# Depthwise convolution of a Conformer layer: three channel blocks on TensorE in place of four, and VectorE's taps dealt anew

## The chip, the cores and the metric

One NeuronCore of a Trainium2 chip runs the whole program as one launch. The metric is the device time of that launch in microseconds (us), the median of a few runs. The engines are TensorE (PE, with its weight loads PEld), VectorE (DVE), ScalarE (ACT), GpSimd (POOL) and SyncE (SP), which here only issues DMAs. Each engine has a queue of its own and works through it in order; engines wait for each other through semaphores.

## The reference

The program is one inference step of a two-layer decoder trunk for 512 prompt rows and 8 x 4 sample rows, 544 rows in all, 1024 channels wide, in float32. Layer 0 is a gated short convolution beside a dilated attention, layer 1 a Conformer convolution module, and each layer ends with a mixture of experts (32 experts, 2 per row). The change lies in the Conformer module:

```python
def odd_mixer(h, w_pw1, b_pw1, dw_w, dw_b, ln_g, ln_b, w_pw2, b_pw2, conv_buf):
    z = h @ w_pw1 + b_pw1
    za, zg = jnp.split(z, 2, axis=-1)
    u = za * jax.nn.sigmoid(zg)
    ctx = jnp.zeros((n, C_KERNEL - 1, C_WIDTH), u.dtype) if conv_buf is None else conv_buf.astype(u.dtype)
    u_ext = jnp.concatenate([ctx, u], axis=1)
    c = causal_dwconv(u_ext, dw_w) + dw_b          # 31 taps, each channel by itself
    c = jax.nn.silu(layer_norm(c, ln_g, ln_b))
    return c @ w_pw2 + b_pw2, u_ext[:, -(C_KERNEL - 1):]
```

## The kernel before

Channels lie on the 128 partitions in eight blocks of 128 (c = 0 to 7), rows along the free axis. The Conformer module follows the experts of layer 0 and the norm after them (`norm(2)`). It goes unit by unit, one unit for each channel block. All queues are written out by hand; nothing reorders them.

**A unit.** TensorE makes two products of 16 `mm` calls each (32 recorded matmuls): m = 2c, the gate, into psum banks 0 and 1, and m = 2c + 1, the value, into banks 2 and 3 (L1814; `z_done` counts them). Product m waits until the banks' earlier content is read: an even one for ScalarE's sigmoid of the unit before (L904, `sig_ready`), an odd one for VectorE's `glu` of the unit before (`u_ready`). `glu(c)` (L1333, L1335, L1337) writes the gated rows u of block c into `cu` (prompt) and `cs` (samples).

**The convolution of the 512 prompt rows** is done in one of two ways.

- *On VectorE*, for the blocks in `DVE_CONV`: ScalarE makes tap 0 with the bias (`first_tap`, L896), and `conv(c, lo, hi)` adds taps lo to hi - 1, one `scalar_tensor_tensor` over 128 x 512 for each (L1351), each waiting for the one before it. `DVE_TAPS[u]` says which taps VectorE does after `glu(u)`; after them it does `sample_sums(u)`, then `glu(u + 1)`.
- *On TensorE*, for the blocks in `PE_CONV`: GpSimd writes 31 small diagonal matrices (`make_diags`, L652), `conv_parts(n)` multiplies with them in 32 x 32 tiles into psum banks 4 to 7 (L1777, 248 recorded matmuls, `part_done`), ScalarE copies the four partial sums out (`keep_parts`, L885, 128 x 2048, `part_kept`), `fold_parts(n)` adds them (L1787, `pe_conv_done`), and ScalarE writes the result with the bias (`keep_pe_conv`, L890, `pe_conv_kept`).

**The sample rows** of every block: GpSimd multiplies windows by taps (L666), VectorE sums them (`sample_sums`, L1360, `sconv_summed`), ScalarE adds the bias (`keep_sconv`, L878).

**Order.** On TensorE, `conv_parts` stands after an even product m and `fold_parts` after product m + 1; the last block's convolution stands among the `mean` products. ScalarE's loop over units does, in this order: sigmoid of c, `keep_sconv(c - 1)`, then, where c is in `PART_AT`, `keep_parts`, then `first_tap(c)` for a VectorE block, then `keep_pe_conv`. After the loop: `keep_sconv(7)`, `keep_parts(3)`, `keep_pe_conv(3)`.

**After the units.** `mean(k)` (L1795) adds block k to the mean over channels in psum and waits for all of block k (`wait_conv`). `mean_done` lets VectorE subtract the mean (L1375); squares (ScalarE L924, GpSimd L672), `variance` (L1834), root, reciprocal, swish and the second projection (L1602) follow, then the norm, the router and the 32 experts of layer 1.

**SyncE** loads the first two expert weights of layer 1 into ring slots 0 and 1 once all products are done and `part_done` has reached `len(PE_CONV)` (L458), since the diagonal matrices lie in those slots.

Of the kernel before, what the change touches and what calls it, by code (L numbers as in the profile page):

```python
# [31 lines left out]
KD = D // P  # L32
# [18 lines left out]
MSLOTS = SLOTS + 2  # L51
PIECE = 1024
CK = 31
PE_CONV = (1, 4, 6, 7)
DVE_CONV = tuple(c for c in range(KD) if c not in PE_CONV)
PW1_SLOT = (2, 3, 0, 1)
LN_PART = ((256, TOK), (0, 256))
PW2_ORDER = (4, 2, 3, 0, 1)
PART_AT = (2, 5, 7)
DVE_TAPS = (((0, 1, 17),), ((0, 17, 31),), ((2, 1, 25),), ((2, 25, 31), (3, 1, 10)), ((3, 10, 25),),  # L60
            ((3, 25, 31), (5, 1, 19)), ((5, 19, 31),), ())
UP = SEQ + CK - 1
US = DEC_T + CK - 1
KEYS = [128, 256, 64]
# [65 lines left out]
def program(nc, x_in, w_mix0, kv_in, w_out, w_pw1, w_pw2, w_moe, smalls, consts, masks, rows, st_a, st_c,  # L130
            y_out, k_out, v_out, ua_p_out, ua_s_out, uc_p_out, uc_s_out):
    ctx = ExitStack()
    with ctx:
# [3 lines left out]
        def sem(name):  # L137
            return ctx.enter_context(nc.semaphore(name))
# [24 lines left out]
        psum = ctx.enter_context(nc.psum_tensor("psum", [P, 8, 512], F32))  # L163

        def view(off, n, pat=None, parts=P, **dims):
            a = ar[0:parts, off:off + n]
            return a.rearrange(pat, **dims) if pat else a

        ident = cst[:, C_ID:C_ID + P]
        mean_of = cst[:, C_MEAN:C_MEAN + P]  # L170

        def bcast(ap, shape):
            return ap.to_broadcast(shape)
# [65 lines left out]
        mean_done = sem("mean_done")  # L239
# [83 lines left out]
        cT = view(B_C, KD * TOK, "p (k t) -> p k t", k=KD)  # L323
# [63 lines left out]
        def diags(n):  # L387

            o = 4096 + CK * 32 * (n % 2)
            return ring[:, n // 2, o:o + CK * 32].rearrange("p (j c) -> p j c", j=CK)  # L390
# [4 lines left out]
        def wait_conv(eng, k):  # L395

            eng.wait_ge(sconv_kept, k + 1)
            if k in PE_CONV:
                eng.wait_ge(pe_conv_kept, PE_CONV.index(k) + 1)
            else:  # L400
                eng.wait_ge(conv_done, k + 1 - sum(c < k for c in PE_CONV))

# [21 lines left out]
        def _(sp):  # L424
# [19 lines left out]
            def experts(n):  # L444
                for u in (2, 0, 1, 3) if n == 0 else (0, 1, 2, 3):
# [6 lines left out]
                    elif u < 2:  # L452

                        sp.wait_ge(z_done, 2 * KD)
                        sp.wait_ge(part_done, len(PE_CONV))
                    else:
# [57 lines left out]
        def _(pool):  # L514
# [135 lines left out]
            def make_diags(n):  # L650
                o = V_DW + CK * PE_CONV[n]
                nc.gpsimd.tensor_tensor(diags(n), bcast(fold[:, None, :], [P, CK, 32]),  # L652
                                        bcast(sv[:, o:o + CK][:, :, None], [P, CK, 32]), ALU.mult
                                        ).then_inc(diag_made, 1)
# [23 lines left out]
        def _(act):  # L678
# [41 lines left out]
            for m in range(23):  # L720
# [8 lines left out]
                if m == 16:  # L729

                    for q in range(4):
                        t = nc.scalar.activation(vS[0:SAMPLES, 4, 192 * q:192 * q + 192],
                                                 psum[32 * q:32 * q + 32, b, 0:192], ACT.Copy)
# [141 lines left out]
            def keep_sconv(c):  # L875
                act.wait_ge(sconv_summed, c + 1)
                out = cT[:, c, SEQ:TOK]
                nc.scalar.activation(out, out, ACT.Identity, bias=sv[:, V_DWB + c:V_DWB + c + 1]  # L878
                                     ).then_inc(sconv_kept, 1)

            def keep_parts(n):
                act.wait_ge(part_done, n + 1)
                if n:
                    act.wait_ge(pe_conv_done, n)
                nc.scalar.activation(parts, psum[:, 4:8, :], ACT.Copy).then_inc(part_kept, 1)  # L885

            def keep_pe_conv(n):
                c = PE_CONV[n]
                act.wait_ge(pe_conv_done, n + 1)
                nc.scalar.activation(cT[:, c, 0:SEQ], psum[:, 4, :], ACT.Identity,  # L890
                                     bias=sv[:, V_DWB + c:V_DWB + c + 1]).then_inc(pe_conv_kept, 1)
# [8 lines left out]
            for c in range(KD):  # L900
# [5 lines left out]
                if c:  # L906
                    keep_sconv(c - 1)
                if c in PART_AT:
                    keep_parts(PART_AT.index(c))
                if c in DVE_CONV:  # L910
                    first_tap(c)
                if c in PART_AT:
                    keep_pe_conv(PART_AT.index(c))
            act.wait_ge(u_ready, KD)
            act.dma_start(brow, rows[0:1, :].to_broadcast([P, D])).then_inc(row_in, 16)
            keep_sconv(7)
            keep_parts(3)
            keep_pe_conv(3)

            sq = hT_of(2)  # L920
            lo, hi = LN_PART[0]
# [19 lines left out]
        def _(dve):  # L941
# [422 lines left out]
            for u in range(KD):  # L1364
                glu(u)
                for c, lo, hi in DVE_TAPS[u]:
                    conv(c, lo, hi)
# [41 lines left out]
        def _(pe):  # L1409
            mm, tr = nc.tensor.matmul, nc.tensor.transpose  # L1410
# [52 lines left out]
            for m in range(23):  # L1463
# [13 lines left out]
                if m == 16:  # L1477

                    for k in range(KD):
                        for q in range(4):  # L1480
                            t = mm(psum[32 * q:32 * q + 32, b, 0:192], hT[:, k, SEQ:TOK],
                                   w[:, k, 192 * q:192 * q + 192], start=k == 0, stop=k == KD - 1,
                                   tile_position=(0, 32 * q))
                elif 12 <= m < 16:
                    i = m - 12
                    for h in range(2):
                        for k in range(KD):
                            t = mm(psum[0:ROWS[i], b + h, 0:384], hT[:, k, P * i:P * i + ROWS[i]],  # L1488
                                   w[:, k, 384 * h:384 * h + 384], start=k == 0, stop=k == KD - 1)
                else:  # L1490
                    c = m % 6 if m < 12 else (4, 5, 2, 3, 0, 1)[m - 17]
                    for h in range(2):
                        for k in range(KD):
                            t = mm(psum[:, b + h, 0:HALF], w[:, k, P * c:P * c + P],  # L1494
                                   hT[:, k, HALF * h:HALF * h + HALF], start=k == 0, stop=k == KD - 1)
# [8 lines left out]
            for g in range(GROUPS):  # L1504
                t = tr(psum[0:32, 3, P * g:P * g + P], ps[:, CACHED + 32 * g:CACHED + 32 * g + 32], ident)
# [4 lines left out]
            for bb in range(2):  # L1510
                for s_, (rows_, g) in enumerate([(SAMPLES, g) for g in range(GROUPS)] + VT):
                    for q in range(4):
# [3 lines left out]
                        t = mm(psum[32 * q:32 * q + 32, 4 + bb, 0:256], w, v, start=s_ == 0,  # L1516
                               stop=s_ == GROUPS + 3, tile_position=(0, 32 * q))
            t.then_inc(so_done, 1)
            pe.wait_ge(so_sum, 1)
            for c in range(4):  # L1520
                t = tr(psum[:, 0, P * c:P * c + P], view(A_OS + P * c, P), ident)
# [45 lines left out]
            for n in range(16):  # L1567
# [7 lines left out]
                for t_ in range(w):  # L1575
                    t = tr(psum[:, 3 + t_ // 4, P * (t_ % 4):P * (t_ % 4) + P], sc[:, P * t_:P * t_ + P], ident)
# [190 lines left out]
            def conv_parts(n):  # L1767

                c = PE_CONV[n]
                pe.wait_ge(u_ready, c + 1)  # L1770
                pe.wait_ge(diag_made, n + 1)
                if n:
                    pe.wait_ge(pe_conv_kept, n)
                for j in range(CK):
                    s = j % 4
                    for i in range(4):
                        t = mm(psum[32 * s:32 * s + 32, 4 + i, :], diags(n)[32 * i:32 * i + 32, j, :],  # L1777
                               cu[32 * i:32 * i + 32, c, j:j + SEQ], start=j < 4, stop=j >= CK - 4,
                               tile_position=(32 * i, 32 * s))
                t.then_inc(part_done, 1)  # L1780

            def fold_parts(n):

                pe.wait_ge(fold_made, 1)
                pe.wait_ge(part_kept, n + 1)
                for i in range(4):
                    t = mm(psum[32 * i:32 * i + 32, 4, :], fold, parts[:, i, :], start=True, stop=True,  # L1787
                           tile_position=(0, 32 * i))
                t.then_inc(pe_conv_done, 1)

            def mean(k):

                wait_conv(pe, k)
                for h, (lo, hi) in enumerate(LN_PART):
                    t = mm(psum[:, h, 0:hi - lo], mean_of, cT[:, k, lo:hi], start=k == 0, stop=k == KD - 1)  # L1795
                return t

            for m in range(2 * KD):
                c, gate = m // 2, m % 2 == 0
                b = 2 * (m % 2)  # L1800
                if m % 4 == 0:
                    pe.wait_ge(dense_w[m // 4], 32)
                slot1 = PW1_SLOT[m // 4]
                if m >= 2:
                    p = m - 2
                    if p % 2 == 0:
                        pe.wait_ge(sig_ready, p // 2 + 1)
                    else:
                        pe.wait_ge(u_ready, p // 2 + 1)
                w = ring[:, slot1, 0:4096].rearrange("p (k c) -> p k c", k=KD)  # L1810
                o = (256 if gate else 0) + P * (c % 2)
                for h in range(2):
                    for k in range(KD):
                        t = mm(psum[:, b + h, 0:HALF], w[:, k, o:o + P], hT2[:, k, HALF * h:HALF * h + HALF],  # L1814
                               start=k == 0, stop=k == KD - 1)
                t.then_inc(z_done, 1)
                if m in (4, 10, 14):
                    conv_parts((4, 10, 14).index(m))
                if m in (5, 11, 15):
                    fold_parts((5, 11, 15).index(m))  # L1820

            pe.wait_ge(sig_ready, KD)
            for k in range(6):
                mean(k)
            conv_parts(3)
            mean(6)
            fold_parts(3)
            mean(7).then_inc(mean_done, 1)
            def variance(h):

                lo, hi = LN_PART[h]
# [147 lines left out]
```

## Time and profile before

| | |
|---|---|
| median of 3 runs | 1252.81 us (1250.18 to 1253.29) |
| the profiled execution | 1254.29 us, its span 1252.5 us, granted TensorE clock 0.939 |
| busy in the span | PE 1082.8 us, DVE 381.4 us, ACT 228.4 us, POOL 190.0 us |
| the first to the last product of the units | 658.9 to 811.7 us |
| VectorE begins to subtract the mean | 832.20 us |

Times in the rows are us from the start of the span; a row of a timeline gives the start, the duration, the engine, the line, the operation, what it writes and reads, and how many instructions are merged in it. In brackets stands for how long the engine was idle before the row, and whose end it then followed. Matmuls are pipelined and their ends are modelled.

### The profile page before, as it was taken

To read this page: it belongs to the slowest core of one execution; us is meant where nothing else is said; L and a number is where in the kernel's file an instruction comes from. 1 tells how busy PE (TensorE), PEld (TensorE's weight loads), DVE (VectorE), ACT (ScalarE), POOL (GpSimd) and SP (SyncE) were. 2 spreads that over 40 slices of the span, in tenths; PEclk is the share of its full clock that TensorE was granted. 3 is DMA by queue.
4 is the path that set the end of the run, shared out by engine and by line. 5 is a ranking of instruction groups with operands and counts; after the bars stand their busy time and mean duration, and the time that the engine had idled before them with its cause. 6 is when DMAs were issued, how large, how long until landed. Compare 5 with 4: busy or idle time off the path is not lost.

```text
span 1252.5 us, 18870 instructions
## 1 busy us (share of the span) xinstructions
PE 1082.8 (86%) x7107; PEld 681.9 (54%) x7108; DVE 381.4 (30%) x733; ACT 228.4 (18%) x413; POOL 190.0 (15%) x301
## 2 busy tenths in 40 slices
PE   5999998899869988888849999989959989798890
PEld 3887585676435544444438776754435545454440
DVE  2000003342351111111154899833262211111116
ACT  4000011344201111101140101144111111011112
POOL 0000010110013222111101211120004322232110
PEclk9999999899988999989979999999979999899895
DMA  9323032800455999999971110070095999989735
GB/s 363 167 95 140 9 117 70 301 2 5 158 220 194 409 408 409 408 405 408 379 286 36 69 67 1 3 259 21 33 391 178 408 408 398 364 330 407 292 151 229
DMA packets 72080, 281.74 MB, mean 225 GB/s; under 512 B 11775, under 2 KB 11839, under 8 KB 68737
## 3 DMA queue, kind: packets, MB, share of 16 engines
q1 hardware_dynamic: 55824, 251.66, 51.4%
q0 software_dynamic: 10960, 17.89, 4.1%
q10 hardware_dynamic: 5216, 11.10, 2.5%
q8 instruction: 54, 0.88, 0.3%
q14 instruction: 26, 0.20, 0.0%
HBM read 270.36 MB, written 29.65 MB: 240 GB/s over the span
## 4 chain that ended last, share of the span: by engine, by line
PE 56%; DMA 24%; DVE 12%; ACT 4%; issue 3%; DVEq 0%; POOL 0%; ACTq 0%; SPq 0%; POOLq 0%
DMA ring<-w_moe 15%; PE psum L1494 11%; PE psum L1683 8%; DMA ar<-w_moe 7%; PE psum L1602 5%; PE psum L1814 5%; DVE ar L1351 4%; PE psum L1738 4%; PE psum L1488 3%; PE psum L1777 3%; PE psum L1711 2%; PE psum L1545 2%; PE psum L1561 1%; PE psum L1666 1%; DVE ar L1138 1%
## 5 line engine op out<-in xcount | busy, mean ns | idle before, releaser
L1683 PE MATMUL psum<-ring,ar 128*64 128x256 f32 x1408 | 179.0, 400 | 21.1 <-DMA ring<-w_moe 19.3
L1683 PEld LDWEIGHTS psum<-ring,ar 128*64 128x64 f32 x1408 | 102.3, 143 | 95.2 <-issue 31.2
L1494 PE MATMUL psum<-ar,ring 128*128 128x272 f32 x576 | 132.7, 393 | 0.0
L1814 PE MATMUL psum<-ar,ring 128*128 128x272 f32 x512 | 120.8, 398 | 3.0 <-DVE ar L1337 3.0
L1494 PEld LDWEIGHTS psum<-ar,ring 128*128 128x128 f32 x576 | 109.3, 190 | 22.9 <-issue 0.3
L1814 PEld LDWEIGHTS psum<-ar,ring 128*128 128x128 f32 x512 | 97.9, 192 | 27.9 <-issue 4.2
L1351 DVE SCALAR_TENSOR_TENSOR ar<-ar,sv 128x512 f32<-128x512 f32 x120 | 107.0, 893 | 5.8 <-ACT ar L896 1.9
L1280 DVE COPY ar<-psum 128x128 f32<-128x128 f32 x64 | 18.6, 291 | 263.0 <-PE psum L1728 252.5
L1683 PE MATMUL psum<-ar 128*64 128x256 f32 x640 | 84.8, 411 | 13.2 <-DMA ar<-w_moe 13.2
L1738 PE MATMUL psum<-ring,ar 128*64 128x512 f32 x352 | 84.1, 598 | 0.8 <-DVE ar L1280 0.4
L1602 PE MATMUL psum<-ring,ar 128*128 128x512 f32 x192 | 84.0, 594 | 0.0
L1683 PEld LDWEIGHTS psum<-ar 128*64 128x64 f32 x640 | 47.6, 146 | 48.8 <-DMA ar<-w_moe 17.6
L619 POOL DMA_INDIRECT expert_outputs<-ar,ixy x64 | 63.8, 996 | 55.9 <-POOL ixy L616 54.7
L819 ACT ACTIVATE ar<-psum 128x128 f32<-128x128 f32 x64 | 17.8, 277 | 250.4 <-PE psum L1683 250.4
L828 ACT ACTIVATE ar<-psum 128x512 f32<-128x512 f32 x64 | 38.2, 597 | 128.1 <-PE psum L1738 128.1
L1602 PEld LDWEIGHTS psum<-ring,ar 128*128 128x128 f32 x192 | 35.9, 190 | 42.6 <-issue 42.5
L1424 PE MATMUL psum<-cst,ar 128*128 128x128 f32 (+1 forms) x160 | 21.4, 280 | 39.3 <-ACT ar L711 32.6
L1262 DVE TENSOR_TENSOR ar<-psum,sv 128x512 f32<-128x512 f32 x64 | 41.2, 686 | 32.1 <-PE psum L1666 32.1
L1273 DVE TENSOR_TENSOR ar<-ar,psum 128x128 f32<-128x128 f32 x64 | 18.4, 288 | 103.4 <-ACT ar L819 103.4
L1008 DVE TENSOR_TENSOR ar<-psum,ar 128x272 f32<-128x272 f32 x2 | 0.9, 442 | 159.7 <-PE psum L1494 159.7
L1432 PE MATMUL psum<-cst 128*128 128x384 f32 x126 | 47.6, 525 | 0.0
L1424 PEld LDWEIGHTS psum<-cst,ar 128*128 128x128 f32 (+1 forms) x160 | 18.2, 149 | 49.3 <-ACT ar L711 32.5
(219 smaller groups left out, 1162.6 us busy)
## 6 DMA issues: line engine op xcount, KB each, us to landing
ring<-w_moe SPq DMA_DIRECT2D x44, 3072.0 KB, 16.9
ar<-w_moe SPq DMA_DIRECT2D x20, 3072.0 KB
ring<-w_mix SPq DMA_DIRECT2D x4, 3072.0 KB, 20.8
ring<-w_pw SPq DMA_DIRECT2D x6, 2048.0 KB, 11.0
ring<-expert_outputs SPq DMA_DIRECT2D x8, 1024.0 KB, 7.9
ring<-kv_in SPq DMA_DIRECT2D x2, 2880.0 KB, 11.7
normed_rows<-ar ACTq DMA_DIRECT2D x8, 512.0 KB, 2.6
X<-x_in ACTq DMA_DIRECT2D x4, 512.0 KB, 9.7
```

The lines of the kernel that those rows point to most:

```text
L619: pool.indirect_dma_start(ys_dram, bass.IndirectOffsetOnAxis(ixy[:, b:b + 1], 0), yj[b], None, bounds_check=4 * TOK - 1, oob_is_err=False) ...
L828: nc.scalar.activation(yj[b], psum[:, 4 + u % 2, :], ACT.Copy).then_inc(moe.y_kept, 1)
L1262: nc.vector.tensor_tensor(xt[:, 4 * h:4 * h + 4, :], psum[:, 3 + 4 * h, :].rearrange("p (k t) -> p k t", k=4), bcast(g[:, :, None], [P, 4, ...
L1351: t = nc.vector.scalar_tensor_tensor(out=out, in0=src, scalar=w, in1=out, op0=ALU.mult, op1=ALU.add)
L1424: t = tr(psum[:, turn_bank(call, s, h), P * k:P * k + r], xn_of(call)[0:r, i, P * (4 * h + k):P * (4 * h + k) + P], ident[0:r, 0:r])
L1432: mm(psum[:, bank, 0:C_SM], ident, cst[:, 0:C_SM], start=True, stop=True)
L1488: t = mm(psum[0:ROWS[i], b + h, 0:384], hT[:, k, P * i:P * i + ROWS[i]], w[:, k, 384 * h:384 * h + 384], start=k == 0, stop=k == KD - 1)
L1494: t = mm(psum[:, b + h, 0:HALF], w[:, k, P * c:P * c + P], hT[:, k, HALF * h:HALF * h + HALF], start=k == 0, stop=k == KD - 1)
L1602: t = mm(psum[0:r, b + h, :], src[:, k, P * i:P * i + r], weights(k, h), start=k == 0, stop=k == blocks - 1)
L1683: t = mm(psum[64 * f:64 * f + 64, u % 2, 0:2 * P], xt[:, k, 64 * (u % 2):64 * (u % 2) + 64], w[:, k, f, :], start=k == 0, stop=k == KD - 1)
L1738: t = mm(psum[64 * h:64 * h + 64, 4 + u % 2, :], aT[:, 64 * k:64 * k + 64], slot(u % MSLOTS)[:, o:o + 512], start=k == 0, stop=k == 1)
L1814: t = mm(psum[:, b + h, 0:HALF], w[:, k, o:o + P], hT2[:, k, HALF * h:HALF * h + HALF], start=k == 0, stop=k == KD - 1)
```

## The change

TensorE convolves blocks 2, 4 and 7 in place of 1, 4, 6 and 7. VectorE convolves blocks 0, 1, 3, 5 and 6, 150 taps in place of 120, and they are dealt anew over the units. The two convolutions within the units come after products 6 and 12 (before: 4, 10 and 14), their folds after 7 and 13, and ScalarE's copies belong to units 3 and 6. Behind the last unit ScalarE serves the TensorE block first and the last sample rows after it, and the mean takes block 6 last.

```diff
-PE_CONV = (1, 4, 6, 7)
+PE_CONV = (2, 4, 7)
 DVE_CONV = tuple(c for c in range(KD) if c not in PE_CONV)
...
-PART_AT = (2, 5, 7)
-DVE_TAPS = (((0, 1, 17),), ((0, 17, 31),), ((2, 1, 25),), ((2, 25, 31), (3, 1, 10)), ((3, 10, 25),),
-            ((3, 25, 31), (5, 1, 19)), ((5, 19, 31),), ())
+PART_AT = (3, 6)
+DVE_TAPS = (((0, 1, 16),), ((0, 16, 31),), ((1, 1, 27),), ((1, 27, 31), (3, 1, 12)), ((3, 12, 28),),
+            ((3, 28, 31), (5, 1, 24)), ((5, 24, 31), (6, 1, 9)), ((6, 9, 31),))
...
             act.wait_ge(u_ready, KD)
             act.dma_start(brow, rows[0:1, :].to_broadcast([P, D])).then_inc(row_in, 16)
+            keep_parts(2)
+            keep_pe_conv(2)
             keep_sconv(7)
-            keep_parts(3)
-            keep_pe_conv(3)
...
-                    t = mm(psum[:, h, 0:hi - lo], mean_of, cT[:, k, lo:hi], start=k == 0, stop=k == KD - 1)
+                    t = mm(psum[:, h, 0:hi - lo], mean_of, cT[:, k, lo:hi], start=k == 0, stop=k == 6)
...
-                if m in (4, 10, 14):
-                    conv_parts((4, 10, 14).index(m))
-                if m in (5, 11, 15):
-                    fold_parts((5, 11, 15).index(m))
+                if m in (6, 12):
+                    conv_parts((6, 12).index(m))
+                if m in (7, 13):
+                    fold_parts((7, 13).index(m))
...
             for k in range(6):
                 mean(k)
-            conv_parts(3)
-            mean(6)
-            fold_parts(3)
-            mean(7).then_inc(mean_done, 1)
+            conv_parts(2)
+            fold_parts(2)
+            mean(7)
+            mean(6).then_inc(mean_done, 1)
```

## Rows read from the trace of the kernel before

**Rows 1.** Timeline of TensorE, the units and the end of the mean.

```profile
658.91 36.83 PE L1814 MATMUL psum<-ar,ring 128*128 128x272 f32 x160
695.67 8.63 PE L1777 MATMUL psum<-ar,ring 32*32 32x512 f32 x248
...
712.76 22.27 PE L1814 MATMUL psum<-ar,ring 128*128 128x272 f32 x96
737.98 16.62 PE L1814 MATMUL psum<-ar,ring 128*128 128x272 f32 x64 [2.95 <-DVE ar L1337]
...
772.11 1.07 PE L1787 MATMUL psum<-ring,cst 128*32 128x512 f32 x8 [0.74 <-ACT ring L885]
...
812.66 5.77 PE L1795 MATMUL psum<-ar,cst 128*128 128x288 f32 x24
...
831.00 1.16 PE L1795 MATMUL psum<-ar,cst 128*128 128x288 f32 x4 [0.89 <-ACT ar L890]
```

**Rows 2.** Timeline of VectorE, units 0 to 7 and the first subtraction.

```profile
673.78 0.50 DVE L1333 SCALAR_TENSOR_TENSOR ar<-psum,sv,ar 128x272 f32<-128x272 f32 x1 [16.51 <-PE psum L1814]
...
692.34 0.49 DVE L1333 SCALAR_TENSOR_TENSOR ar<-psum,sv,ar 128x272 f32<-128x272 f32 x1
...
711.87 0.50 DVE L1333 SCALAR_TENSOR_TENSOR ar<-psum,sv,ar 128x272 f32<-128x272 f32 x1 [3.01 <-PE psum L1814]
...
714.11 21.39 DVE L1351 SCALAR_TENSOR_TENSOR ar<-ar,sv 128x512 f32<-128x512 f32 x24 [0.95 <-ACT ar L896]
735.54 1.19 DVE L1360 TENSOR_REDUCE ar<-ar 128x32 f32<-128x992 f32 x1
736.64 0.49 DVE L1333 SCALAR_TENSOR_TENSOR ar<-psum,sv,ar 128x272 f32<-128x272 f32 x1
...
737.84 14.90 DVE L1351 SCALAR_TENSOR_TENSOR ar<-ar,sv 128x512 f32<-128x512 f32 x15
...
753.88 0.49 DVE L1333 SCALAR_TENSOR_TENSOR ar<-psum,sv,ar 128x272 f32<-128x272 f32 x1
...
755.07 13.55 DVE L1351 SCALAR_TENSOR_TENSOR ar<-ar,sv 128x512 f32<-128x512 f32 x15
...
771.41 0.50 DVE L1333 SCALAR_TENSOR_TENSOR ar<-psum,sv,ar 128x272 f32<-128x272 f32 x1 [1.57 <-PE psum L1814]
...
794.24 0.49 DVE L1333 SCALAR_TENSOR_TENSOR ar<-psum,sv,ar 128x272 f32<-128x272 f32 x1
...
806.52 1.18 DVE L1360 TENSOR_REDUCE ar<-ar 128x32 f32<-128x992 f32 x1
...
832.20 5.65 DVE L1375 TENSOR_TENSOR ar<-ar,psum 128x288 f32<-128x288 f32 x16 [15.67 <-PE psum L1795]
```

**Rows 3.** Chain that ended last: three taps of unit 2 (20 equal ones between).

```profile
715.68 2.51 DVE ar L1351
...
718.21 0.76 DVE ar L1351
...
734.75 0.76 DVE ar L1351
```

**Rows 4.** Timeline of GpSimd, the sample product of unit 4.

```profile
755.23 2.60 POOL L666 TENSOR_TENSOR ar<-ar,sv 128x992 f32<-128x992 f32 x1 [12.37 <-DVE ar L1337]
```

**Rows 5.** Timeline of ScalarE in unit 5: sample rows, then the partial sums.

```profile
769.88 0.32 ACT L878 ACTIVATE ar<-ar,sv 128x32 f32<-128x32 f32 x1 [14.53 <-DVE ar L1360]
770.10 1.86 ACT L885 ACTIVATE ring<-psum 128x2048 f32<-128x2048 f32 x1
```

**Rows 6.** Windows: busy us of PE, PEld, DVE, ACT, POOL; then clock, DMA share, GB/s.

```profile
738.00:746.00 8.00, 8.00 (x28) 6.33 (x29) 7.82 (x7) 1.37 (x2) 4.86 (x2) 0.79 0.00 0
827.00:835.00 8.00, 5.14 (x24) 2.91 (x25) 2.80 (x8) 4.88 (x9) 0.00 (x0) 1.00 0.86 313
928.00:936.00 8.00, 7.66 (x19) 4.89 (x20) 6.56 (x28) 0.21 (x1) 0.00 (x0) 0.67 1.03 409
```

**Rows 7.** Timeline of TensorE, the first product behind a long wait in the router.

```profile
928.34 0.90 PE L1641 MATMUL psum<-ar,cst 128*128 128x160 f32 x2 [7.83 <-DVE ar L1183]
```

## The prediction

> **What bounds the kernel now.** I read the page's busy shares and its chain first, then the timelines of TensorE and VectorE through the eight units, the chain in the same stretch, the waits, and last the granted clock in short windows. In the units two engines take turns. TensorE's products run at 22.27 / 3 = 7.42 us each, its convolution of one block takes 8.6 us from start to next start, its fold 1.0 [rows 1]. VectorE's unit is `glu`, taps and the sample sum. From where one `glu` begins to where VectorE is free for the next I read, for units 0 to 6: 18.56, 16.43, 24.77, 17.24, 15.87, 22.83 and 13.38 us [rows 2]. (Unit 1 is 711.87 - 3.01 - 692.34, less the 0.09 by which a `glu` starts ahead of the sum's end, 735.54 + 1.19 against 736.64; unit 4 likewise; unit 6 is 806.52 + 1.10 - 794.24.) Where a `glu` begins at once, VectorE sets the pace (units 1, 3, 4, 6); where its row shows a wait for L1814, TensorE does: 3.01 us before unit 2 and 1.57 before unit 5 [rows 2]. Both engines have slack of a few us at most, so work moved from one to the other is worth neither its full length nor nothing: the wait at each crossing has to be followed.
>
> **Prices.** A free tap takes 0.76 us and comes every (734.75 - 718.21) / 21 = 0.788 [rows 3]. Taps that meet a GpSimd product of 2.60 us [rows 4] stretch: 15 taps of unit 4 took 13.55 where 15 x 0.788 = 11.82, so 1.73 for each unit's sample product; the 15 of unit 3, where GpSimd also wrote diagonal matrices, took 14.90, so 1.35 more [rows 2]. One tap shows this directly with 2.51 us [rows 3].
>
> **The change on VectorE.** Thirty taps more. Unit by unit, at 0.788 a tap:
> unit 0, 15 taps for 16: 17.77. Unit 1, 15 for 14: 17.22. Unit 2, 26 for 24, and its first tap belongs to block 1, whose tap 0 ScalarE made a unit earlier, so the 0.95 wait on ScalarE [rows 2] goes: 25.43. Unit 3, 16 for 15, without diagonal matrices, as only three sets are made: 16.68. Unit 4, 16 for 15: 16.66. Unit 5, 26 for 24: 24.40. Unit 6, 15 for 12: 15.74. Unit 7 has 22 taps where it had none; by unit 4 with seven taps more, 21.38. Together 155.3 us from 673.78, so 829.1 if VectorE never waited.
>
> **The change on TensorE.** One convolution and one fold less: 8.6 + 1.0 = 9.6 us of work. Products 0 to 4 are as before, to 695.7; 5 ends at 703.1, 6 at 710.5. `glu(2)` starts at 673.78 + 17.77 + 17.22 = 708.77 and is done before the convolution of block 2 wants it at 710.5; that ends at 719.1, product 7 at 726.5.
>
> **The step that decides: the first fold.** TensorE's next instruction is `fold_parts(0)`, and it needs ScalarE's `keep_parts(0)`. In ScalarE's queue that stands behind `keep_sconv(2)`, which waits for the sample sum at the end of VectorE's unit 2. Before, the fold in unit 5 began 2.27 us after VectorE's sum had ended (769.84 to 772.11), through the two copies [rows 1, 2, 5]. Now the sum of unit 2, with its 26 taps, ends at 708.77 + 25.43 + 0.09 = 734.3, so the fold begins at 736.6: TensorE stands for 10 us, with products 8 and 9 queued behind it. The copies before had the same order, but the unit before the fold was then a short one, and the waits at the folds were at most 0.74 [rows 1]. Fold and two products, 1.0 + 14.85, end at 752.4. VectorE is free at 734.2 + 16.68 = 750.9 and waits 1.6 for `glu(4)`.
>
> The second fold repeats it. Unit 4 ends at 769.1, product 11 at 767.3, so `glu(5)` is not late. Unit 5 has 26 taps and ends at 793.5. TensorE has done 12, the convolution of block 4 and 13 by 790.7 and waits for 793.6 + 2.27 = 795.9, so 5.2 us. Fold, 14 and 15 end at 811.7; VectorE is free at 793.5 + 15.74 = 809.3 and waits 2.5. Unit 7 then ends at 811.8 + 21.4 = 833.2.
>
> **The clock.** A wait of 2.95 us before product 9 was followed by a granted clock of 0.79 over 8 us, and the two products took 16.62 in place of 14.85 [rows 1, 6]: 0.21 x 8 = 1.7 us lost, that is, some us at the lower of the two levels, 1.2 GHz. After a wait of 7.83 us [rows 7] it was 0.67 over 8 us, 2.6 us lost [rows 6]. The products behind the folds are what VectorE waits for, so this is on the path. I take 2.1 for each of the two folds, the middle of 1.7 and 2.6: 4.2 in all. The Trainium skill (TensorE: Matmul & The Clock Gate, Part 1) says that the gate's point of change is not tied to the kernel's start and falls elsewhere from run to run; by that the price of one and the same wait would differ between executions, and the sum would lie anywhere between that without and that with the loss. The rows have a wait of 2.95 that cost 1.7, and also several together of about 3 us in 827 to 835 with a clock of 1.00 [rows 6], which I use as the lower bound of the third wait, below.
>
> **The end.** The last sample sum ends at 833.3 + 4.2 = 837.5. ScalarE's `keep_sconv(7)` (0.35 with its start) and TensorE's start (0.15) put `mean(7)` at 838.0. `mean(6)` follows; at 1.16 for one [rows 1] less their overlap both take 2.1, so VectorE subtracts from 840.1, against 832.20 [rows 2]: +7.9. Meanwhile TensorE does `mean(0)` to `mean(5)` (5.8 us [rows 1]) from 815.9, the last convolution and the fold by 833.4; it then waits 4.6 us. The clock may fall for the two means and the variance behind them: 0 to 1.7, I take 0.9. That is +8.8.
>
> **What costs nothing.** ScalarE's new order at the end is hidden: its copies for block 7 are done near 834, before the sum it defers. Taking block 6 last in the mean is hidden too, as its last tap ends one sample sum ahead of 837.5. `first_tap(3)` stands behind `keep_parts(0)` and ends at about 737.4; VectorE reaches it after four taps of block 1, near 740.3; if that cover went, the price would be 0.8. GpSimd's missing fourth set of diagonal matrices lies in unit 3, where it is counted above. SyncE's loads of the first expert weights, queued behind `part_done`, start some 3 us later than now while everything that uses them moves by 8.8. Behind the subtraction nothing changes, and no transfer started before it sets the end, so the delay goes through to the end one for one.
>
> **Sum.** 1.6 + 2.5 + 4.2 of waits on VectorE, and 829.1 as the unhindered end, give 837.5 for the last sum, +7.9 at the subtraction and +8.8 with the last clock loss. The profiled execution, 1254.3, would become 1263.1; it lay 1.5 above the median, so the median becomes 1252.8 + 8.8 = 1261.6.
>
> **Rivals.** Within 0.3% (3.8 us) a measurement here cannot tell from no change.
> (a) *The folds stall, the clock costs little.* Then only 1.6 + 2.5 of waits remain, and the subtraction is at 840.1 - 4.2 = 835.9: +3.7 with nothing lost, up to +6 where one of the three waits is punished. For it: the windows' price varies. Against: both waits before a fold are longer than the 2.95 that was punished. 1256.5 to 1258.8.
> (b) *VectorE's taps meet GpSimd less.* This is the way to a time that is not slower. Six sample products and three matrix writes lie in units on the path (0, 1, 2, 4, 5, 7): 6 x 1.73 + 3 x 1.35 = 14.4 us. From three products gone the change is within 0.3% (8.8 - 5.2 = +3.6); with nearly all gone, TensorE's 9.6 us less would show and the time be 1247. Against: both engines still start from the same `u_ready`, as in every unit before. About 1256 if a third goes.
> (c) *VectorE runs through without waiting for TensorE.* 829.1 leads to a subtraction at 831.8, so -0.4: 1252.4. It needs the ten-us wait at the first fold to be absent; the queue order above speaks against it.
> (d) *Worse.* Longer spells at the lower clock, 2.6 at each fold and 1.7 at the end, with heavier collisions in the long units: +11.5 and more, 1264.5 to 1267.
>
> **Chances and range.** My forecast, +6 to +11.5, 0.66; (a) 0.13; (b) 0.08; (c) 0.05; (d) 0.08. The forecast itself reaches from 3.7 + 2 x 1.7 = 7.1 to 3.7 + 2 x 2.6 + 1.7 = 10.6, and 1 us more each way for the unit lengths. The range takes in most of (a) below and the start of (d) above: 1256.5 to 1264.8. Slower by over 0.3% is my forecast, (d) and most of (a): 0.84. Within 0.3%: the rest of (a) and most of (b) and (c): 0.12. Faster: 0.04.
>
> **What would show it.** Right: TensorE idle about 10 us before the first L1787 and about 5 before the second, with L885 as releaser; L878 and L885 back to back near 734.5; VectorE waiting for L1814 before its fifth and eighth L1333 (3.7 and 4.6 us with the clock loss); a granted clock under 1 just behind both folds; 150 instructions of L1351; the subtraction near 840. Wrong: if the folds start within 2 us of the product before them, the step on ScalarE's queue has failed; if the clock stays 1.00 behind them, (a) holds; if units 2 and 5 last under 24 and 23 us, (b). If the subtraction is at 840 but the end is not 8 to 9 us later, some transfer behind it took the delay up, which I have excluded.

## The result, and the profile after

| | before | after |
|---|---|---|
| median of 8 executions each | 1254.77 us (1250.18 to 1264.04) | 1266.88 us (1260.33 to 1273.26) |
| ratio of the executions | 1 | 1.0084, 95% interval 1.0049 to 1.0119 |
| profiled execution, its span | 1254.29, 1252.5 us | 1273.26, 1271.5 us |
| first product of the units (L1814) | 658.91 | 664.48 |
| VectorE begins to subtract the mean (L1375) | 832.20 | 848.09 |
| first reciprocal (L1379) | 837.90 | 855.70 |

The change makes the kernel slower by 0.5 to 1.2%. The direction was forecast and the size was too small: 1261.6 us and a range to 1264.8, against 1266.88. Timed again, with 12 executions beside 29 of before, the ratio was 1.0072 (1.0045 to 1.0098).

One stretch is compared in all that follows: **T, from the first product to the first reciprocal**. It is 837.90 - 658.91 = 178.99 us before and 855.70 - 664.48 = 191.22 after, so 12.2 more (the rows of before are below). It repeats: two more profiles of the changed kernel gave 191.53 and 191.14. What lies outside it does not repeat so well. Over all 17 profiles of this study the first product came at 656.4 to 665.1 us, and the span ended 410.7 to 418.2 us after the first reciprocal. None of the kernels has a change there. Of the 19.0 us between the two profiled spans, 12.2 are T, 5.6 the later first product and 1.2 the rest; only T holds edited instructions. The later first product goes with the granted clock between 200 and 300 us, in a stage that no edit touches: 0.86, 0.86 and 0.88 in the three profiles of the changed kernel, 0.93 before. It repeats with the kernel, and why is open.

T is read from profiled executions, and these were not the typical ones. Those of the changed kernel took 1273.26, 1272.31 and 1268.81 us, all above its two medians of 1266.88 and 1266.55. In timed executions the growth is known only to about 6 to 15 us, and 6 to 12 in the second timing, which is what the intervals above come to.

TensorE's timeline after, from the first convolution to the variance, answers to [rows 1]:

```profile
715.91 8.62 PE L1777 MATMUL psum<-ar,ring 32*32 32x512 f32 x248
724.46 7.60 PE L1814 MATMUL psum<-ar,ring 128*128 128x272 f32 x32
742.70 1.93 PE L1787 MATMUL psum<-ring,cst 128*32 128x512 f32 x8 [10.64 <-ACT ring L885]
744.57 38.20 PE L1814 MATMUL psum<-ar,ring 128*128 128x272 f32 x160
782.70 8.62 PE L1777 MATMUL psum<-ar,ring 32*32 32x512 f32 x248
791.25 7.60 PE L1814 MATMUL psum<-ar,ring 128*128 128x272 f32 x32
804.22 1.93 PE L1787 MATMUL psum<-ring,cst 128*32 128x512 f32 x8 [5.37 <-ACT ring L885]
806.09 16.16 PE L1814 MATMUL psum<-ar,ring 128*128 128x272 f32 x64
...
838.81 1.49 PE L1787 MATMUL psum<-ring,cst 128*32 128x512 f32 x8 [2.06 <-ACT ring L885]
844.06 3.99 PE L1795 MATMUL psum<-ar,cst 128*128 128x288 f32 x8 [3.76 <-ACT ar L878]
849.07 6.06 PE L1834 MATMUL psum<-ar,cst 128*128 128x288 f32 x16 [1.02 <-ACT ar L924]
```

The two brackets of 10.64 and 5.37 us are TensorE standing before a fold. Both end with ScalarE's copy L885. The last two rows are the two means and the variance: 3.99 and 6.06 us, for two means that were reckoned at 2.1 and a variance that took 4.15 before. The kernel before, the variance, the first reciprocal and the window around them:

```profile
833.18 4.15 PE L1834 MATMUL psum<-ar,cst 128*128 128x288 f32 x16 [1.02 <-ACT ar L924]
...
837.90 1.95 DVE L1379 RECIPROCAL ar<-ar 128x288 f32<-128x288 f32 x1
...
833.00:841.00 8.00, 7.37 (x26) 4.85 (x26) 7.91 (x19) 6.17 (x12) 5.18 (x9) 1.00 1.02 415
```

ScalarE's timeline after the change says why L885 was late:

```profile
740.48 0.32 ACT L878 ACTIVATE ar<-ar,sv 128x32 f32<-128x32 f32 x1 [23.75 <-DVE ar L1360]
740.70 1.86 ACT L885 ACTIVATE ring<-psum 128x2048 f32<-128x2048 f32 x1
...
802.00 0.32 ACT L878 ACTIVATE ar<-ar,sv 128x32 f32<-128x32 f32 x1 [18.48 <-DVE ar L1360]
802.22 1.86 ACT L885 ACTIVATE ring<-psum 128x2048 f32<-128x2048 f32 x1
```

The copy follows at once on the sample rows of the unit before, and those had waited 23.75 us for VectorE's sum. TensorE's partial sums had been ready at 715.91 + 8.62 = 724.5.

VectorE's timeline after, the units around the folds and the end:

```profile
714.33 0.49 DVE L1333 SCALAR_TENSOR_TENSOR ar<-psum,sv,ar 128x272 f32<-128x272 f32 x1
...
715.53 23.69 DVE L1351 SCALAR_TENSOR_TENSOR ar<-ar,sv 128x512 f32<-128x512 f32 x26
739.25 1.19 DVE L1360 TENSOR_REDUCE ar<-ar 128x32 f32<-128x992 f32 x1
740.36 0.49 DVE L1333 SCALAR_TENSOR_TENSOR ar<-psum,sv,ar 128x272 f32<-128x272 f32 x1
...
760.81 0.50 DVE L1333 SCALAR_TENSOR_TENSOR ar<-psum,sv,ar 128x272 f32<-128x272 f32 x1 [4.60 <-PE psum L1814]
...
822.29 0.50 DVE L1333 SCALAR_TENSOR_TENSOR ar<-psum,sv,ar 128x272 f32<-128x272 f32 x1 [4.60 <-PE psum L1814]
...
842.47 1.18 DVE L1360 TENSOR_REDUCE ar<-ar 128x32 f32<-128x992 f32 x1
848.09 5.66 DVE L1375 TENSOR_TENSOR ar<-ar,psum 128x288 f32<-128x288 f32 x16 [4.44 <-PE psum L1795]
855.70 1.95 DVE L1379 RECIPROCAL ar<-ar 128x288 f32<-128x288 f32 x1 [1.96 <-ACT ar L927]
```

From its first `glu` to the end of its last sum, 679.35 to 843.65, VectorE is busy for 148.4 of 164.3 us. Its long waits are the two of 4.60 us, for the products queued behind the folds. Windows behind the two folds and from the two means on; the clock is the third number from the right:

```profile
742.70:750.70 8.00, 8.00 (x29) 5.17 (x30) 7.75 (x9) 1.25 (x2) 1.63 (x1) 0.72 0.00 0
804.20:812.20 8.00, 7.98 (x29) 5.16 (x30) 7.75 (x9) 1.27 (x2) 1.60 (x1) 0.72 0.01 2
844.00:856.00 12.00, 10.92 (x28) 7.48 (x29) 5.95 (x17) 5.09 (x12) 4.50 (x8) 0.63 0.86 347
```

One less the clock, times the length, is the time lost: 2.2 us behind each fold and 4.4 in the last window, of which not all is on the path. In slices of 1 us the clock is at the lower level until about 747.2 behind the first fold and 808.6 behind the second, 4.4 us each from where the fold begins. At the end it is there from 839.3 to 853.0, through both means and most of the variance.

### The profile page after: what moved, and what is told of

Read it like the earlier page. It is cut to its first block, busy times and chain, and to the rows that moved or that the text cites. A ratio compares the mean times of both kernels' runs of the same rounds, so it can differ in the third digit from the quotient of the medians.

```text
span 1271.5 us, 18385 instructions
## 1 busy us (share of the span) xinstructions
PE 1083.5 (85%) x6851; PEld 680.2 (53%) x6852; DVE 404.8 (32%) x763; ACT 226.9 (18%) x412; POOL 188.6 (15%) x300
## 4 chain that ended last, share of the span: by engine, by line
PE 51%; DMA 24%; DVE 17%; ACT 5%; issue 3%; DVEq 0%; POOL 0%; ACTq 0%; SPq 0%; POOLq 0%
DMA ring<-w_moe 14%; PE psum L1494 10%; PE psum L1683 8%; DVE ar L1351 8%; DMA ar<-w_moe 7%; PE psum L1602 5%; PE psum L1738 4%; PE psum L1814 4%; PE psum L1488 3%; PE psum L1545 2%; PE psum L1711 2%; DVE X L1098 1%; PE psum L1561 1%; PE psum L1666 1%; DVE ar L1138 1%
## 5 line engine op out<-in xcount | busy, mean ns | idle before, releaser
L1351 DVE SCALAR_TENSOR_TENSOR ar<-ar,sv 128x512 f32<-128x512 f32 x150 | 130.4, 871 | 5.9 <-ACT ar L896 1.0
L1814 PE MATMUL psum<-ar,ring 128*128 128x272 f32 x512 | 121.1, 399 | 0.0
L1814 PEld LDWEIGHTS psum<-ar,ring 128*128 128x128 f32 x512 | 98.7, 194 | 25.7 <-issue 5.0
```

The lines of the kernel that those rows point to most:

```text
L1351: t = nc.vector.scalar_tensor_tensor(out=out, in0=src, scalar=w, in1=out, op0=ALU.mult, op1=ALU.add)
```

## The experiments

All start from the changed kernel unless said otherwise. In kernels whose line numbers moved, L1813 is the products, L1776 the convolution, L1786 the fold, L1794 the mean, L1374 the subtraction and L1378 the reciprocal.

| kernel | T | ratio of executions to before, interval |
|---|---|---|
| before | 178.99 | 1 |
| after, three profiles | 191.22, 191.53, 191.14 | 1.0084 (1.0049 to 1.0119), 1.0072 (1.0045 to 1.0098) |
| copies first | 181.87 | 1.0004 (0.9981 to 1.0026) |
| flat deal of the taps | 181.95 | 1.0019 (0.9998 to 1.0041) |
| end filled, two profiles | 187.75, 187.36 | 1.0044 (1.0013 to 1.0074) |
| all waits filled, 12 and 6 calls | 184.87 | 1.0084 (1.0056 to 1.0112) |
| the same, 14 and 7 calls, four profiles | 183.42, 183.19, 183.18, 183.21 | 1.0082 (1.0050 to 1.0113) |
| the same, 7 and 3 calls | 186.84 | 1.0050 (1.0026 to 1.0074) |
| copies first, end filled | 178.05 | 0.9982 (0.9960 to 1.0005) |
| before, taps even, copies first, new tail | 173.15 | 0.9966 (0.9943 to 0.9990) |
| before, taps even, copies first | 179.64 | 0.9993 (0.9970 to 1.0016) |

**Copies first.** ScalarE serves the fold before the sample rows of the unit before:

```diff
-                if c:
-                    keep_sconv(c - 1)
                 if c in PART_AT:
                     keep_parts(PART_AT.index(c))
+                    keep_pe_conv(PART_AT.index(c))
+                if c:
+                    keep_sconv(c - 1)
                 if c in DVE_CONV:
                     first_tap(c)
-                if c in PART_AT:
-                    keep_pe_conv(PART_AT.index(c))
```

> The measure is T, from TensorE's first product of the units (L1814) to the first reciprocal of the deviation (L1379): 178.99 us before, 191.22 after the change. This kernel is the changed one with ScalarE's keep_parts and keep_pe_conv ahead of keep_sconv in units 3 and 6. Theory A (the folds wait behind VectorE's long units only through ScalarE's queue): the two waits before the first two folds fall from 10.6 and 5.4 us to under 2, VectorE runs its eight units without waiting for a product, its last sum ends 170.2 us after the first product; the last fold now leaves TensorE idle for some 8 us, so its clock loss at the end (up to 3.8 us) stays. T = 178.6 to 182.4, the whole time from 0.4 us below to 3.4 us above the kernel before. Theory B (150 taps in place of 120 are the cost by themselves, or TensorE waits for VectorE's glu anyway): T stays at 188 or more.

T was 181.87, inside the expectation. TensorE's timeline of this kernel around the first fold, and at the end:

```profile
720.94 7.60 PE L1813 MATMUL psum<-ar,ring 128*128 128x272 f32 x32
728.47 1.06 PE L1786 MATMUL psum<-ring,cst 128*32 128x512 f32 x8
729.46 7.60 PE L1813 MATMUL psum<-ar,ring 128*128 128x272 f32 x32
738.14 14.94 PE L1813 MATMUL psum<-ar,ring 128*128 128x272 f32 x64 [1.08 <-DVE ar L1336]
...
831.15 4.00 PE L1794 MATMUL psum<-ar,cst 128*128 128x288 f32 x8 [4.12 <-ACT ar L878]
```

The fold follows the product with no bracket, TensorE now waits within the units only 0.8 to 1.5 us at a time for VectorE, and VectorE goes from unit to unit without standing: its last sum ends at 829.57 + 1.18, 169.8 us after the first product (the expectation's 170.2), after the change 179.2. The means still take 4.00 us. With the same 150 taps T is 9.4 us less, so theory B falls.

**A flat deal**, queues as they are:

```diff
-            ((0, 16, 31),), ((1, 1, 27),), ((1, 27, 31), (3, 1, 12)), ((3, 12, 28),),
-            ((3, 28, 31), (5, 1, 24)), ((5, 24, 31), (6, 1, 9)), ((6, 9, 31),))
+            ((0, 16, 31),), ((1, 1, 17),), ((1, 17, 31), (3, 1, 13)), ((3, 13, 29),),
+            ((3, 29, 31), (5, 1, 15)), ((5, 15, 31), (6, 1, 10)), ((6, 10, 31),))
```

> The changed kernel with its queues as they are and the same 150 taps dealt as 15, 15, 16, 26, 16, 16, 25, 21 over the units, so that the unit ahead of each of the two folds (2 and 5) is short. Theory A: the waits at the folds fall from 10.6 and 5.4 us to 2 and 3.5, VectorE waits for no product, and T falls from 191.2 to 179 to 183. Theory B (number of taps or TensorE's order sets it): the same number of taps in the same blocks gives 188 or more.

T was 181.95, and the two waits 2.75 and 2.21 us for an expected 2 and 3.5. The two folds and the product behind the first, in TensorE's timeline of this kernel:

```profile
731.34 1.94 PE L1787 MATMUL psum<-ring,cst 128*32 128x512 f32 x8 [2.75 <-ACT ring L885]
733.21 37.47 PE L1814 MATMUL psum<-ar,ring 128*128 128x272 f32 x160
...
788.97 1.94 PE L1787 MATMUL psum<-ring,cst 128*32 128x512 f32 x8 [2.21 <-ACT ring L885]
```

So either half of the coupling, the queue order or the long unit ahead of the fold, can be undone and the loss in the units is gone. The folds themselves ran in 1.94 us where [rows 1] have 1.07, so even waits of 2.75 and 2.21 us were followed by the lower clock, but VectorE had work enough to cover it.

**The waits filled.** TensorE still holds the fold back as long as before, but passes the time with products (`stay_warm`) into a psum bank that is free at that moment:

```diff
                 if m in (7, 13):
+                    pe.wait_ge(sig_ready, m // 2 + 1)
+                    stay_warm(12 if m == 7 else 6)
                     fold_parts((7, 13).index(m))
...
             conv_parts(2)
+            stay_warm(2, 2)
             fold_parts(2)
+            stay_warm(5, 2)
             mean(7)
```

> The changed kernel with TensorE's waits filled by products whose result is not used: 12 calls (8.4 us) ahead of the first fold, 6 (4.2 us) ahead of the second, 2 ahead of and 5 behind the third. The waits themselves stay. Theory A (waits of about 1.6 and 2.5 us on VectorE, the rest of the loss is the granted clock): granted clock 1.00 behind the folds, VectorE's waits before its fifth and eighth glu fall from 4.6 each to about 2 and 2.5, T falls by about 2.5 at each of the folds and 3.8 at the end, to 182 to 184. Rival C (the clock is incidental, the stall itself is the cost): T stays within 2 us of 191.2.

T was 184.87, just above the expected 182 to 184, since 2.89 us of the first wait stayed and cost a spell at the lower clock. With 14 and 7 calls:

> The changed kernel with the three waits filled further: 14 calls for 12 ahead of the first fold, 7 for 6 ahead of the second. With 12, TensorE still stood 2.89 us before the first fold, the clock fell for 3.4 us, and VectorE waited 4.14 us there and 2.50 at the second, where the clock had held. Theory A: with the first wait filled too, VectorE waits 1.6 to 2.4 there and 2.5 at the second, T = 183 to 183.5, and the whole time is 4 to 5 us above before, ratio 1.003 to 1.004. The run with 12 had T = 184.87 in its profile but a ratio of 1.0084, no better than without filling. Rival E: filling costs in other executions what it gains in the profiled one (it runs at half rate and overshoots when the clock is down), and the ratio stays near 1.008.

Windows of the kernel with 14 and 7 calls, behind the two folds and behind the two means, then VectorE's waits before its fifth and eighth `glu`:

```profile
737.40:745.40 8.00, 7.95 (x38) 5.99 (x39) 7.75 (x9) 1.29 (x2) 1.68 (x1) 1.00 0.00 0
796.80:804.80 8.00, 7.97 (x38) 5.99 (x39) 7.75 (x9) 1.27 (x2) 1.61 (x1) 1.00 0.00 0
836.00:848.00 12.00, 10.19 (x62) 5.91 (x61) 10.84 (x25) 8.75 (x17) 5.18 (x9) 1.00 0.85 339
```

```profile
753.42 0.50 DVE L1333 SCALAR_TENSOR_TENSOR ar<-psum,sv,ar 128x272 f32<-128x272 f32 x1 [2.46 <-PE psum L1814]
...
812.79 0.50 DVE L1333 SCALAR_TENSOR_TENSOR ar<-psum,sv,ar 128x272 f32<-128x272 f32 x1 [2.50 <-PE psum L1814]
```

The clock is 1.00 in all three windows and the waits are 2.46 and 2.50. Against the 4.60 each of the unfilled kernel, the clock was 2.1 us of either wait, in the profile.

**The end alone.**

> The changed kernel with only the third wait filled (2 calls ahead of the last fold, 5 behind it). If the end alone cost 3.8 us by the clock (two means 3.99 us where 2.1 was reckoned, variance 6.06 where it took 4.15), T is 187.4, the two means take about 2.1 us and the variance 4.15; if the clock at the end is not the cause, T stays at 191.

> The changed kernel with only the third wait filled, timed. Its profile had T = 187.75 against 191.22 and 191.53. If the end's clock loss is in the unprofiled executions too, it is 3 to 4 us faster than the changed kernel timed beside it. If filling works in the profile alone, the two are equal within 0.2%.

T was 187.75 and 187.36. The timed executions were 0.28% below those of the changed kernel timed beside it (1.0044 against 1.0072), some 3.5 us, but the two intervals overlap (1.0013 to 1.0074, 1.0045 to 1.0098): the timed executions agree with the profile and do not show it by themselves. In the profile of the timed one the two means took 2.10 us and the variance 4.15:

```profile
839.71 2.10 PE L1795 MATMUL psum<-ar,cst 128*128 128x288 f32 x8 [1.04 <-ACT ar L878]
842.83 4.15 PE L1836 MATMUL psum<-ar,cst 128*128 128x288 f32 x16 [1.02 <-ACT ar L924]
```

**Where the filling's gain went.** The fully filled kernels' profiles were 8 us shorter in T, but their timed executions had ratios of 1.0084 and 1.0082, as without filling. I repeated one three times:

> The changed kernel with its three waits filled (14, 7, 2 and 5 calls) once more. Its profile had T = 183.42 and an execution of 1262.67 us, but its four executions had a ratio of 1.0082, as the unfilled kernel. Rival E (in other executions the filling overshoots, so T is larger there): T spreads, 186 to 191 in at least one of three repeats. If the stage is repeatable and the ratio is spread from elsewhere, T = 183 to 185 in all three, and the executions differ outside it.

> Second repeat of the changed kernel with its waits filled: as the first, T = 183 to 185 if the stage repeats, 186 to 191 under rival E.

> Third repeat of the changed kernel with its waits filled: as the first, T = 183 to 185 if the stage repeats, 186 to 191 under rival E.

T was 183.19, 183.18 and 183.21, with executions of 1261.57, 1259.53 and 1255.33 us: in profiles the stage repeats to 0.3 us. All four profiled executions lie at or below 1262.67 us, while the ratio 1.0082 comes from four executions with a median of 1266.02. Then half the filling, and the changed kernel beside it:

> The changed kernel with all three waits filled, the two before the folds with half as much (7 and 3 calls, 4.9 and 2.1 us of the 10.6 and 5.4). An overshooting filling (rival E) cannot happen here: then this kernel's ratio is 1.003 to 1.006, below the 1.008 of the fully filled ones. If the ratio stays at 1.007 or more, overshooting is not what ate the gain. In the profile the half filled waits leave 5 and 3 us of standing, so the clock may fall as without filling: T = 184 to 188.

> The changed kernel as it is, timed beside the two others: ratio to the kernel before 1.006 to 1.010, T = 191 to 192 in the profile.

> The changed kernel once more, as it is, for a second trace: how far T (191.22) and the three losses by the clock repeat. Expected: VectorE's waits before its fifth and eighth glu 3.5 to 5.5 us each, T = 188 to 193.

Half the filling had T = 186.84 and a ratio of 1.0050, lower than both fully filled kernels, as a filling that overshoots, that is, lasts beyond the moment when the fold could start, would have it. But the intervals overlap, and of the unprofiled executions only time, span and mean clock are on record. The mean clock says one thing: it averaged 0.932 over the 20 executions of the changed kernel, and 0.939 and 0.942 over the 9 and the 4 of the fully filled ones. So the filling seems to have kept the clock up in timed executions too, and to have added time elsewhere; where is open. The half filled kernel stands where filling the end alone does (1.0044), so at the folds no filling gained anything that was timed. It follows that the 2.1 us by the clock at either fold are shown for profiled executions alone; the clock loss at the end is shown in profiles, and the timed executions agree with it.

**Both losses taken out.**

> The changed kernel with ScalarE's copies first, as before, and the third wait filled, so that nothing of the two suspected losses is left. T as before (178.99 us before, 191.22 after the change, 181.87 with the copies first). Theory A: the last sum stays at 168.6 us after the first product, as VectorE's 150 taps without a wait set it; the two means take 2.1 and the variance 4.15, so T = 178 to 178.5 and the whole time is 0.5 us under the kernel before, ratio 0.998 to 1.001. Rival D (the clock loss at the end is made up by something else on the path): T stays at 181 to 182.

T was 178.05, 3.8 less than with the copies first alone, and 0.9 less than before: of T's growth nothing is left, and five blocks on VectorE do as well as the kernel before (0.9982, 0.9960 to 1.0005).

**A version that is faster than both.** Four blocks on TensorE as before, but no long unit anywhere:

```diff
-DVE_TAPS = (((0, 1, 17),), ((0, 17, 31),), ((2, 1, 25),), ((2, 25, 31), (3, 1, 10)), ((3, 10, 25),),
-            ((3, 25, 31), (5, 1, 19)), ((5, 19, 31),), ())
+DVE_TAPS = (((0, 1, 16),), ((0, 16, 30),), ((0, 30, 31), (2, 1, 18)), ((2, 18, 30),), ((2, 30, 31), (3, 1, 17)),
+            ((3, 17, 31), (5, 1, 5)), ((5, 5, 21),), ((5, 21, 31),))
...
-            for k in range(6):
-                mean(k)
+            mean(0)
+            mean(1)
             conv_parts(3)
-            mean(6)
+            mean(2)
+            mean(3)
+            mean(4)
             fold_parts(3)
+            mean(5)
+            mean(6)
```

with the copies first as above.

> The kernel before with its four TensorE blocks, the 120 taps dealt as 15, 14, 18, 12, 17, 18, 16, 10 (before 16, 14, 24, 15, 15, 24, 12, 0), ScalarE's copies ahead of the sample rows, and the last convolution after two of the means with the others behind it. If what costs is a product or a fold that waits for a long unit of VectorE, no product waits here (before: 2.95, 0.61, 0.74, 0.20 us and 1.8 by the clock), the tail loses its two waits of 0.9 on ScalarE, and T = 170 to 173 in place of 178.99: the whole time 6 to 9 us less, ratio 0.993 to 0.995. If the engines' total work set the stage, T stays at 177 to 179.

T was 173.15, 5.8 us less, and the ratio 0.9966 (0.9943 to 0.9990): faster, by less than the 0.993 to 0.995 that was forecast. TensorE's tail in it:

```profile
804.92 1.06 PE L1786 MATMUL psum<-ring,cst 128*32 128x512 f32 x8
805.91 2.10 PE L1794 MATMUL psum<-ar,cst 128*128 128x288 f32 x8
807.94 7.50 PE L1776 MATMUL psum<-ar,ring 32*32 32x512 f32 x209
817.24 2.13 PE L1776 MATMUL psum<-ar,ring 32*32 32x512 f32 x39 [1.79 <-issue]
819.30 3.02 PE L1794 MATMUL psum<-ar,cst 128*128 128x288 f32 x12
822.25 1.07 PE L1786 MATMUL psum<-ring,cst 128*32 128x512 f32 x8
823.25 3.02 PE L1794 MATMUL psum<-ar,cst 128*128 128x288 f32 x12
```

Up to the last mean no bracket names another engine: TensorE works through from its first product, but for 1.79 us in the last convolution. I thought that the new tail carried nothing of it and took it out:

> The kernel before with two of the three edits of the kernel with four blocks dealt evenly (T = 173.15): the even deal of 120 taps and the copies first, but the order of the last convolution, fold and means as before. If the gain of 5.8 us comes from the units alone (product 15 ended at 804.9 after a first product at 658.85, before 811.7 after 658.91) and the new tail gave nothing (from there to VectorE's subtraction 21.3 us, before 20.5), T = 172 to 173 and the ratio 0.993 to 0.998. If the new tail carried part of it, T = 174 to 175.

That was wrong. T was 179.64 and the ratio 0.9993, no gain. The units end as early (the third fold at 805.20), but in the old order `mean(5)` stands ahead of the convolution and now waits for block 5's last taps, which the even deal put into unit 7:

```profile
816.27 2.15 PE L1794 MATMUL psum<-ar,cst 128*128 128x288 f32 x4 [5.23 <-DVE ar L1350]
818.35 9.50 PE L1776 MATMUL psum<-ar,ring 32*32 32x512 f32 x248
```

It is the fault of the change itself in small: taps moved into a later unit, and an instruction that needs them left in front of one that doesn't. Behind that wait the mean took 2.15 us where one of before took 1.18, and the convolution 9.50 for 8.63. What the even deal and the copies first are worth each by itself was not separated.

## Where the prediction was right, and the step that failed

- *The deciding step*, the first fold behind ScalarE's queue: right. Forecast standing 10 and 5.2 us, measured 10.64 and 5.37; copies first removes it and with it the loss in the units.
- *Unit lengths*: unit 2 was 740.36 - 714.33 = 26.03 for 25.43, 0.6 more. The 0.95 wait that fell away had kept VectorE out of the start of GpSimd's matrix write: that write (L652) took 1.86 us in unit 2 before and 2.30 after, as in units 1 and 3, which had no such wait. Unit 3 was a slip: it has 4 + 11 = 15 taps, not 16. As VectorE waits behind it anyway, this only made that wait longer.
- *VectorE's waits*: forecast 3.7 and 4.6 with the clock, measured 4.60 and 4.60. Without the clock 1.6 and 2.5 were forecast, 2.46 and 2.50 measured with the waits filled; the 0.8 of the first is the tap of unit 3.
- *The clock behind the folds*: 2.1 each forecast and 2.1 measured, in the profile. The forecast took the middle of two windows elsewhere in the kernel, so that it fits this closely is in part luck. The price of these waits hardly differed between profiles: VectorE waited 4.60, 4.76 and 4.55 us at the first, 4.60, 4.69 and 4.58 at the second.
- *The last sum*: forecast 837.5 - 658.9 = 178.6 us after the first product, measured 842.47 + 1.18 - 664.48 = 179.2.
- **The term that was mis-sized is the clock loss at the end**: I took 0.9 from a range of 0 to 1.7. The sum's end to the subtraction was 848.09 - 843.65 = 4.4 us for the 2.6 reckoned, and the subtraction to the reciprocal 7.6 for the 5.7 of before: 1.8 + 1.9 = 3.7. Filling this wait alone gave back 3.5 to 3.8 us in T, and the timed executions agree. The bound of 1.7 came from one short window with two products at full stretch [rows 6]; here the lower clock lasted from 839.3 to 853.0, 8.9 us of it from where the means begin, against 4.4 from where either of the other folds begins. It fell during the last fold, behind a wait of 2.06 us on ScalarE and ahead of one of 3.76. The wait of 1.02 before the variance is no cause by itself: it stands in the kernel before and with the end filled too, where the variance took 4.15. Why the spell is so long where the means and the variance follow one another was not tried. With 3.7 for 0.9 and 0.6 for unit 2 the forecast's 8.8 becomes 12.2, which is T's growth.
- *The range* was also made against a single profile and a median of three. With eight executions the kernel before stood at 1254.77, 2 us higher; the first product alone wanders by 9 us between profiles. So of the 5.3 us between 1261.6 and 1266.88, 2.0 are this base and 3.3 the growth. The forecast's growth, 8.8 us or 0.70%, lies within both measured intervals: that the end's clock was taken too low is shown by T, and the timed growth alone would not have told. My rival (d), more time at the lower clock, with a chance of 0.08, gave 1264.5 to 1267 and holds the measured median. Its place was the end, not the folds.
- *Rivals (a), (b), (c)* fell: the clock did fall at all three places, the taps met GpSimd as before, and VectorE ran through without waiting only once the folds were freed.
- *Nothing behind the subtraction took the delay up*: the span after the reciprocal was 415.8 us, and 413.8 and 412.9 in the two other profiles, against 414.6 before.

## What to carry to other kernels

When work moves between two engines that take turns, follow what the third one has in its queue: a copy that waits in order behind another engine's long stretch makes the producer of its data stand too. Before moving a convolution, a fold or some taps, list for each instruction what stands ahead of it that waits for something later. Deal such work evenly first, and count a wait of TensorE twice: once for itself, and once for the slower products after it. Here the second part was 2.1 us behind each fold among long products, and 3.7 where two means and a variance followed.

## What the hardware showed beyond that

- Waits of 2.75 and 2.21 us before a fold were enough to have the fold itself run at half rate (1.94 us for 1.07), while [rows 6] has a window with 2.9 us of standing in pieces and a clock of 1.00.
- In the last convolution TensorE stood in mid-run with nothing to wait for that the profile shows: 1.79 us in the tail above, 2.75 with copies first, 3.10 with the flat deal, 0.22 in the changed kernel, none before. They were long where the convolution began soon after the output transfers (L502) were issued: 0.0 us behind them with copies first, 0.2 with the flat deal and 1.6 in the tail above, but 4.1 in the changed kernel and 5.3 before. Whether the transfers are the cause was not tried.
